# Moving the context's layer-1 top-k and the latents' filter into another stage, and pairing the latents' attention on the two halves of TensorE, in a two-layer backbone step

## The chip, the cores and the metric

The kernel runs on one NeuronCore of a Trainium2 chip. The metric is the device time of one execution in microseconds (us); lower is better. Below, DVE is VectorE, ACT is ScalarE, PE is TensorE's matmul side, POOL is GpSimd and SP is SyncE.

## The reference, cut to what matters

Two streams of tokens go through two layers with the same weights: the context (128 tokens, "C") and the latents (512 tokens, "L"). Layer 1 of a stream needs layer 0 of that stream and nothing of the other one.

```python
def layer(x, mod, P, rope, k_ext, v_ext):          # D=1024, 8 query heads, 2 kv heads, head_dim 64
    h = rmsnorm(x, norm_mix_g) * (1 + sc_m) + sh_m
    proj = h @ w_in
    attn = attention(q, k, v)                      # latents: 128 cached + 512 own keys; context: 128 keys
    hy   = hyena(proj[...], P)                     # long convolution; its filter depends on weights alone
    sg   = chunk_gmlp(proj[...])
    x = x + g_m * (concat([attn, hy, sg]) @ w_out)
    h = rmsnorm(x, norm_ffn_g) * (1 + sc_f) + sh_f
    return x + g_f * peer(h, ...)

def peer(h, wq, keys, u_tab, v_tab):               # 8 heads, 128 keys a half, top 16
    q = (h @ wq).reshape(T, 8, 2, 64)
    s = einsum('thpd,hpnd->thpn', q, keys)         # two rows of 128 scores per token and head
    s_top, i_top = top_k(s, 16)                    # of each half
    cand = s_top[..., 0, :, None] + s_top[..., 1, None, :]       # 16 x 16
    sc, pos = top_k(cand, 16)
    idx = i_top0[pos // 16] * 128 + i_top1[pos % 16]
    gate = softmax(sc)
    a = gelu(einsum('td,ted->te', x, u_tab[idx]))  # 128 rows of 4 KB per token from u_tab
    return einsum('te,ted->td', gate * a, v_tab[idx])            # and 128 from v_tab
```

The filter is `sin(fr2*(sin(fr1*(feats@fw1+fb1))@fw2+fb2))@fw3`, times an exponential, and its spectrum.

## The kernel before, in words

All engines follow one list, `ORDER`, that is worked out when the program is built; each engine does, in that order, what a job gives it, and waits on semaphores between. There are two kinds of jobs.

*Mixer jobs* are everything up to the scores: `rms`, `app` (norm and modulation), `f1`, `f2`, `f3`, `hf` (the filter: two sines, the taps, the spectrum), `qk`, `vt`, `hy`, `su` (projections), `rot`, `sp`, `df`, `cv`, the attention jobs `as` (scores), `at` (turning the probabilities with a diagonal matrix of 1/sum, line 823) and `av` (values, line 835), then `wo`, `wq`, and `ka`, `kb` (the two halves of the keys, line 865).

*Expert jobs* work in units. A unit is one head of one tile of 128 tokens, and in a unit each of the 128 partitions handles one token and its 16 experts. Step `u` of a group does for unit `u` 16 `dot` jobs (DVE, line 1415: a gathered row of u_tab times the token), for unit `u-1` 16 `add` jobs (the gathered row of v_tab times a weight), and for unit `u+1` the `pick` jobs, which are the top-k chain on DVE (lines 1358 to 1402, 27 instructions, each waiting for the one ahead). In the context's groups `add` is a DVE instruction (line 1429). In the latents' groups it is two matmuls with a diagonal matrix that ACT makes (lines 885 and 1113). Rows are gathered by POOL (line 610), one indirect DMA of 128 rows of 4 KB each, u and v in turn, into rings of four places each (`rows_ring`); a place is free when its `dot` or `add` is done.

The groups are context layer 0 (8 units), latents layer 0 (32), context layer 1 (8) and latents layer 1 (32). `weave` puts expert jobs between mixer jobs in proportion to a table `ROOM` of costs per mixer job. So the program has these stages:

1. context mixer of layer 0, alone;
2. latents mixer of layer 0, woven with the experts of context layer 0;
3. context mixer of layer 1, woven with steps 0 to 16 of latents layer 0;
4. steps 17 to 32 of latents layer 0, alone, and then `start_jobs(2)`: the picks of the first unit of context layer 1;
5. latents mixer of layer 1, woven with the experts of context layer 1. It begins `rms app f1 f2 f3 f3 f3 f3 hf hf hf hf qk ...`;
6. latents experts of layer 1, alone, and the outputs.

Weights come in blocks of 1 MB through a ring of four places that SP fills in the order in which they are used.

A softmax unit of the latents is one head of one tile of 128 queries: `n // (2 * NT)` is the pair of heads, and the half of the partitions (0 to 63 or 64 to 127) changes only every four units. Three units are in flight, each in two PSUM banks. `ROOM` gives 9 to each `as`, `at` and `av`, which is 864 for the 32 units; the whole list is 2964 in layer 0 and 3004 in layer 1.

## Time and profile before

| | |
|---|---|
| median of 3 runs | 4240.7 us (4236.87 to 4241.16) |
| the profiled execution, its own time | 4239.37 us |
| span of its instructions | 4237.5 us |
| mean granted TensorE clock (share of 2.4 GHz) | 0.934 |
| DVE busy in the span | 2951.7 us (70%) |
| PE busy | 3274.7 us (77%) |
| POOL busy | 2563.5 us (60%) |
| ACT busy | 1065.3 us (25%) |
| moved by DMA | 1485.64 MB, mean 351 GB/s |

The shares of busy time are means over six stages with different limits, so they say little by themselves. The windows of the profile, which give busy times and GB/s for stretches of the span, are what to read here.

### The profile page before, as it was taken

Reading aid. Unit: us, or ns where it says so; the run is one execution under the profiler, and the core shown is the slowest. Engines: PE = TensorE matmul, PEld = TensorE weight load, DVE = VectorE, ACT = ScalarE, POOL = GpSimd, SP = SyncE. Lnnn points to the kernel's source line nnn. Section 1 sums busy time; section 2 is a strip of 40 time slices with the busy share of each in tenths; the row PEclk is TensorE's granted clock in tenths of the full one; section 3 lists DMA queues with packets and bytes.
Section 4 is the critical chain, followed back from the end, with each engine's and each line's share of the span. In section 5 each row is a group of like instructions: output and inputs, shape, how many; then the busy total and the mean of one; then the engine's idle time right before and its main releaser. Section 6 shows DMA issues by size and latency. Waiting matters only on the chain.

```text
span 4237.5 us, 33926 instructions
## 1 busy us (share of the span) xinstructions
PE 3274.7 (77%) x9680; PEld 1513.7 (36%) x9680; DVE 2951.7 (70%) x6826; ACT 1065.3 (25%) x2256; POOL 2563.5 (60%) x2564
## 2 busy tenths in 40 slices
PE   6797896577778787777776978975777777777777
PEld 4653653233333333222222536542222222222223
DVE  2388998545667666677764889897676767677673
ACT  4322322122222222222223323221222222222222
POOL 0054666345656666777773545566777777777774
PEclk8898998689999999999998988987999999999999
DMA  7587788899989999999995877788999999999998
GB/s 281 215 314 276 262 297 287 330 378 369 381 332 384 379 407 386 408 409 401 409 407 191 318 277 244 275 303 336 409 407 395 407 409 400 409 406 401 401 409 313
DMA packets 394007, 1485.64 MB, mean 351 GB/s; under 512 B 44124, under 2 KB 46878, under 8 KB 377952
## 3 DMA queue, kind: packets, MB, share of 16 engines
q0 software_dynamic: 368640, 1342.34, 82.5%
q1 hardware_dynamic: 25184, 141.13, 8.6%
q8 instruction: 81, 1.33, 0.1%
q14 instruction: 102, 0.84, 0.1%
HBM read 1480.42 MB, written 2.88 MB: 350 GB/s over the span
## 4 chain that ended last, share of the span: by engine, by line
DMA 25%; DVE 21%; PE 19%; POOL 18%; issue 13%; ACT 4%; SPq 0%; DVEq 0%; ACTq 0%; POOLq 0%
POOL rows_ring L610 18%; DMA rows_ring<-in_peer_u,idx 13%; DMA rows_ring<-in_peer_v,idx 11%; PE psum L885 8%; DVE rows_ring L1415 7%; DVE mix L1429 4%; PE psum L700 4%; PE psum L687 1%; PE psum L823 1%; DVE small L1334 1%; PE psum L656 1%; DMA ring<-in_ada 1%; DVE pos L1362 1%; DVE pos L1359 1%; DVE cand L1360 1%
## 5 line engine op out<-in xcount | busy, mean ns | idle before, releaser
L885 PE MATMUL psum<-rows_ring,diag 128*128 128x512 f32 x4096 | 2042.7, 627 | 674.9 <-DMA rows_ring<-in_peer_v,idx 544.5
L610 POOL DMA_INDIRECT rows_ring<-in_peer_u,idx x1280 | 1298.0, 1014 | 1015.5 <-DVE rows_ring L1415 475.3
L1415 DVE SCALAR_TENSOR_TENSOR rows_ring<-rows_ring,psum 128x1024 f32<-128x1024 f32 x1024 | 1240.7, 1220 | 678.9 <-DMA rows_ring<-in_peer_u,idx 639.7
L610 POOL DMA_INDIRECT rows_ring<-in_peer_v,idx x1280 | 1265.2, 988 | 634.2 <-issue 306.6
L885 PEld LDWEIGHTS psum<-rows_ring,diag 128*128 128x128 f32 x4096 | 717.3, 193 | 1937.6 <-DMA rows_ring<-in_peer_v,idx 1231.7
L1113 ACT ACTIVATE diag<-ident,wts 128x128 f32<-128x128 f32 x1024 | 382.3, 397 | 1333.3 <-PE psum L885 1332.6
L700 PE MATMUL psum<-area,ring 128*128 128x128 f32 (+1 forms) x1344 | 386.7, 447 | 15.6 <-ACT area L975 14.9
L1429 DVE SCALAR_TENSOR_TENSOR mix<-rows_ring,wts,mix 128x1024 f32<-128x1024 f32 x254 | 326.4, 1285 | 15.5 <-DMA rows_ring<-in_peer_v,idx 13.9
L1415 DVE SCALAR_TENSOR_TENSOR rows_ring<-rows_ring,area 128x1024 f32<-128x1024 f32 x256 | 311.9, 1222 | 13.5 <-DMA rows_ring<-in_peer_u,idx 12.0
L700 PEld LDWEIGHTS psum<-area,ring 128*128 128x128 f32 x1344 | 216.3, 200 | 195.0 <-issue 191.7
L700 PE MATMUL psum<-mix,ring 128*128 128x128 f32 (+1 forms) x512 | 143.0, 441 | 2.9 <-DVE mix L1354 2.1
L1105 ACT ACTIVATE acts<-dots 128x16 f32<-128x16 f32 x80 | 17.3, 216 | 498.4 <-DVE rows_ring L1415 498.3
L823 PE MATMUL psum<-sg_junk,area 128*128 128x128 f32 x672 | 109.5, 314 | 37.0 <-DVE sg_junk L1343 37.0
L823 PEld LDWEIGHTS psum<-sg_junk,area 128*128 128x128 f32 x672 | 93.5, 214 | 53.8 <-DVE sg_junk L1343 43.5
L1101 ACT ACT_TABLE_LOAD x75 | 96.2, 1283 | 41.0 <-DVE wts L1440 41.0
L700 PEld LDWEIGHTS psum<-mix,ring 128*128 128x128 f32 x512 | 80.8, 198 | 67.3 <-issue 63.6
L835 PE MATMUL psum<-area,v_tok 128*64 128x128 f32 x672 | 102.4, 304 | 0.0
L1075 ACT ACTIVATE area<-psum,small 128x640 f32<-128x640 f32 (+1 forms) x80 | 56.9, 711 | 176.0 <-DVE small L1334 175.9
L1105 ACT ACT_TABLE_LOAD x78 | 100.1, 1283 | 1.4
L813 PE MATMUL psum<-area 64*128 64x512 f32 x128 | 81.6, 720 | 13.3 <-ACT area L1082 6.7
L1082 ACT COPY area<-psum 128x640 f32<-128x640 f32 (+1 forms) x80 | 48.5, 606 | 161.3 <-PE psum L823 161.3
L835 PEld LDWEIGHTS psum<-area,v_tok 128*64 128x64 f32 x672 | 81.4, 152 | 15.7 <-issue 9.3
(176 smaller groups left out, 2497.3 us busy)
## 6 DMA issues: line engine op xcount, KB each, us to landing
ring<-in_ada SPq DMA_DIRECT2D x48, 1024.0 KB, 8.2
ring<-in_win SPq DMA_DIRECT2D x32, 1024.0 KB, 8.1
rows_ring<-in_peer_u,idx POOLq DMA_INDIRECT x1280, 7.2
rows_ring<-in_peer_v,idx POOLq DMA_INDIRECT x1280, 7.1
ring<-in_wout SPq DMA_DIRECT2D x16, 1024.0 KB, 8.0
ring<-in_wq SPq DMA_DIRECT2D x16, 1024.0 KB, 7.8
ring<-in_dft SPq DMA_DIRECT2D x12, 1024.0 KB, 7.8
xT<-in_xT_in SPq DMA_DIRECT2D x1, 2048.0 KB, 13.1
```

What stands on the lines that cost most here:

```text
L610: pool.indirect_dma_start(row(table, k), None, (peer_u, peer_v)[table], bass.IndirectOffsetOnAxis(ap=idx[u % IDX_PLACES][:, k:k + 1], axis ...
L700: m = pe.matmul(g[:, 0:WIDTH[st]], w[:, k * P:(k + 1) * P], src(k), start=(k == 0), stop=(k == KC - 1))
L813: pe.matmul(g[:, 0:512], q, kT[st][rows, 0:512], start=True, stop=True)
L823: m = pe.matmul(att_bank(st, n)[:, b * P:(b + 1) * P], probs[st][:, n % 2, b * P:(b + 1) * P], softmax_diag[:, n % 2, :], start=True, stop ...
L835: m = pe.matmul(out_bank(st, c)[rows, t * P:(t + 1) * P], v_tok[:, b, rows], probsT[st][:, n % 2, i * P:(i + 1) * P], start=(i == 0), stop ...
L885: m = pe.matmul(acc[:, b, :], diag[:, k % 4, :], row(1, k)[:, b * 512:(b + 1) * 512], start=(u % PEER_HEADS == 0 and k == 0), stop=last)
L1075: act.activation(probs[st][:, n % 2, :], att_bank(st, n)[:, 0:KEYS[st]], ACT.Exp, bias=negmax[:, n % 2:n % 2 + 1], accum_out=rowsum[:, n % ...
L1101: act.activation(gate_e[:], best[:], ACT.Exp, bias=gate_s[:, 1:2], accum_out=gate_s[:, 0:1]).then_inc(s["gexp_ready"], 1)
L1105: act.activation(acts[:], dots[:], ACT.Gelu_apprx_tanh).then_inc(s["gelu_ready"], 1)
L1113: act.activation(diag[:, k % 4, :], ident[:], ACT.Copy, scale=wts[:, k:k + 1]).then_inc(s["diag_ready"], 1)
L1415: dve.scalar_tensor_tensor(out=row(0, k), in0=row(0, k), scalar=1.0, in1=h, op0=ALU.mult, op1=ALU.mult, accum_out=dots[:, k:k + 1]).then_i ...
L1429: m = dve.scalar_tensor_tensor(out=out_tok[C_], in0=x, scalar=wts[:, k:k + 1], in1=out_tok[C_], op0=ALU.mult, op1=ALU.add)
```

## The change

It has five parts.

- **Picks ahead.** In steps 18 to 25 of group 1 (latents layer 0) DVE also does the picks of the eight units of group 2 (context layer 1), one unit a step. Group 2 then has none of its own, and `start_jobs(2)` goes. Its indices and gates get places for all eight units.
- **Filter earlier.** `f1 f2 f3 hf` of the latents of layer 1 leave stage 5 and are woven into steps 25 to 32 of group 1, with buffers of their own.
- **Picks in eight parts.** A pick has 24 instructions instead of 27, in eight parts instead of six: the two one-hot halves are now one instruction of 512 elements each. It works on the scores themselves, and ACT's copy of them (`stage`) goes.
- **Attention by pairs.** The latents' softmax units go two at a time, one on each half of the partitions, so that neighbouring matmuls of the scores (64 rows) and of the values (64 columns) lie on different halves of the array. Two pairs are in flight instead of three units. The diagonal matrix of 1/sum moves from DVE to ACT. `ROOM` for it is now 10 + 20 + 10 per pair, 640 in all.
- **Keys by pairs.** `ka` and `kb` are one job on PE, the two halves in turn.

```diff
@@ attention_jobs
+    if st == L_:
+        n = ATT_UNITS[L_] // 2
+        jobs = [("fence", l, st, 0), ("pas", l, st, 0), ("pas", l, st, 1)]
+        for m in range(n):
+            jobs += [("pat", l, st, m)] + ([("pav", l, st, m - 1)] if m else [])
+            jobs += [("pas", l, st, m + 2)] if m + 2 < n else []
+        return jobs + [("pav", l, st, n - 1), ("fence", l, st, 1)]
@@ filter_jobs, mixer_jobs
+FILTER_FROM = 25
+def filter_jobs(l):
+    return [("f1", l, L_, 0), ("f2", l, L_, 0)] + [(k, l, L_, t) for k in ("f3", "hf") for t in range(LAT_TILES)]
-        jobs = js("rms:0 app:0 f1:0 f2:0") if l else []
-        jobs += js("f3:0 f3:1 f3:2 f3:3 hf:0 hf:1 hf:2 hf:3")
+        jobs = js("rms:0 app:0") if l else js("f3:0 f3:1 f3:2 f3:3 hf:0 hf:1 hf:2 hf:3")
@@ step_jobs, expert_jobs, ORDER
-PICK_LINKS = (0, 5, 10, 16, 20, 23, 27)
+PICK_LINKS = (0, 3, 5, 8, 10, 13, 16, 21, 24)
+PICK_AT = (0, 1, 3, 4, 6, 7, 9, 10)
+PICKED_AHEAD = (2,)
+AHEAD_FROM = 18
-        jobs += [("pick", grp, u + 1, p // 2)] if u + 1 < n and p % 2 and p // 2 < PICK_PARTS else []
+        if own and ahead and p < PICK_PARTS:
+            jobs += pick_jobs(grp, u + 1, [p])
+        elif own and not ahead and p in PICK_AT:
+            jobs += pick_jobs(grp, u + 1, [PICK_AT.index(p)])
+        if ahead and p >= PICK_PARTS:
+            jobs += pick_jobs(*ahead, [p - PICK_PARTS])
-    ORDER += expert_jobs(_g, range(_a, UNITS[_g] + 1))
-    if _l + 1 < DEPTH:
-        ORDER += start_jobs(_g + 1)
+        ORDER += expert_jobs(_g, range(_a, FILTER_FROM))
+        _a = FILTER_FROM
+        ORDER += weave(filter_jobs(_l + 1), expert_jobs(_g, range(_a, UNITS[_g] + 1)))
@@ TensorE
+            def pair_scores(l, st, m):
+                if m >= 2:
+                    pe.wait_ge(s["pair_copied"], 2 * done("pat", l, st, m - 2))
+                for n, a, b in ((2 * m, 512, 640), (2 * m + 1, 128, 640), (2 * m, 0, 512), (2 * m + 1, 0, 128)):
+                    c, rows, t = unit_of(st, n)
+                    if (a, b) == (0, 128):
+                        pe.wait_ge(s["pair_first"], done("pas", l, st, m))
+                    ins = pe.matmul(att_bank(st, n)[:, a:b], qT[st][rows, c, t * P:(t + 1) * P], kT[st][rows, a:b], start=True, stop=True)
@@ ScalarE, at "pat": exp of pair m+1, copy of pair m, diagonals of pair m+1
+                    act.activation(probs[st][m % 2][:, n % 2, :], att_bank(st, n), ACT.Exp, bias=negmax[:, n % 2:n % 2 + 1],
+                                   accum_out=rowsum[:, n % 2:n % 2 + 1]).then_inc(s["pair_exp"], 1)
+                    act.copy(probsT[st][:, n % 2, :], att_bank(st, n)).then_inc(s["pair_copied"], 1)
+                    act.activation(softmax_diag[:, n % 2, :], ident[:], ACT.Copy, scale=rinv[:, n % 2:n % 2 + 1]
+                                   ).then_inc(s["pair_diag"], 1)
@@ VectorE, pick
-                if part < 2:
-                    top16(topv[:, part, :], topi[:, part, :], unit_s[:, part, :], step)
+                if part < 4:
+                    half = part // 2
+                    src = scores[st][:, (2 * u + half) * N_KEYS:(2 * u + half + 1) * N_KEYS]
+                    if part % 2 == 0:
+                        top8(vals, idxs, src, step)
+                        step(dve.match_replace(src, vals[:, 0:8], src, -3.0e38))
+                    else:
+                        next8(vals, idxs, src, step)
```

On DVE, the end of stage 4 and the start of stage 5 read so before (`xT` is the last write of the latents' experts, `unit_s` the first unit of group 2, line 1402 its indices, line 1169 the norm, lines 1198 to 1203 the first sine's argument):

```order
L1451 SCALAR_TENSOR_TENSOR xT<-psum,modT,xT 128x128 x8
L1358 MAX topv<-unit_s 128x8
L1359 MAX_INDEX topi<-topv,unit_s 128x8
...
L1400 SCALAR_TENSOR_TENSOR idxf<-picked 128x16
L1402 TENSOR_SCALAR idx<-idxf 128x16
L1169 TENSOR_TENSOR area<-xT,rstd 128x512 x8
L1415 SCALAR_TENSOR_TENSOR rows_ring,dots<-rows_ring,area 128x1024
L1198 TENSOR_SCALAR area<-psum,par 64x512
```

The changed kernel has there (line 1560 is the `dot`, line 1343 the first key's gain):

```order
L1597 SCALAR_TENSOR_TENSOR xT<-psum,modT,xT 128x128 x8
L1289 TENSOR_TENSOR area<-xT,rstd 128x512 x8
L1560 SCALAR_TENSOR_TENSOR rows_ring,dots<-rows_ring,area 128x1024 x2
L1343 TENSOR_SCALAR area<-psum,par 128x512
L1560 SCALAR_TENSOR_TENSOR rows_ring,dots<-rows_ring,area 128x1024 x9
```

The pick of 27 instructions and the filter's instructions are gone from this place, and the norm follows the last write of `xT`.

In step 25 of group 1 the changed kernel's DVE has both additions; `xT` is the last tile's write back, `sq` the second sine's argument, `gate_l` belongs to the latents' own pick:

```order
L1597 SCALAR_TENSOR_TENSOR xT<-psum,modT,xT 128x128 x8
L1490 MAX topv<-area 128x8
...
L1491 MAX_INDEX pos<-best,onehot 128x8
L1318 TENSOR_SCALAR sq<-psum,par 64x512
L1319 TENSOR_SCALAR sq<-sq 64x512
L1320 TENSOR_SCALAR sq<-sq 64x512
L1322 SCALAR_TENSOR_TENSOR sq<-sq 64x512 x3
L1323 TENSOR_SCALAR sq<-sq 64x512
L1560 SCALAR_TENSOR_TENSOR rows_ring,dots<-rows_ring,psum 128x1024
L1531 MATCH_REPLACE onehot<-best,onehot 128x256
```

Before, a step held 16 dots, one pick and `weigh`; steps 18 to 25 now hold 16 dots and two picks, and step 25 also the write back, both sines' arguments and the first of four `f3`.

On PE the latents' attention read before (813 and 814 scores, 823 the turn, 835 the values), one unit after another:

```order
L813 MATMUL psum<-area 128x512
L814 MATMUL psum<-area 128x128
L823 MATMUL psum<-sg_junk,area 128x128 x5
L835 MATMUL psum<-area,v_tok 64x128 x5
L813 MATMUL psum<-area 128x512
```

and now (891 scores, 900 the turn, 913 the values), one pair after another:

```order
L891 MATMUL psum<-area 128x128
L891 MATMUL psum<-area 128x512 x2
L891 MATMUL psum<-area 128x128
L900 MATMUL psum<-sg_junk,area 128x128 x10
L913 MATMUL psum<-area,v_tok 64x128 x10
```

The number of matmuls per unit is the same; what moved is which half of the array neighbours use, and that two units wait and are waited for together.

## Rows read from the trace of the kernel before

**Rows 1.** The page: GB/s that DMA moved, in 40 equal slices.

```profile
GB/s 281 215 314 276 262 297 287 330 378 369 381 332 384 379 407 386 408 409 401 409 407 191 318 277 244 275 303 336 409 407 395 407 409 400 409 406 401 401 409 313
```

**Rows 2.** Windows by stage: stretch, length, each engine's busy us and instructions, clock, DMA.

```profile
core 0: us, PE busy (x) PEld busy (x) DVE busy (x) ACT busy (x) POOL busy (x), PEclk, DMA share, GB/s
207.00:760.00 553.00, 455.49 (x1733) 275.61 (x1733) 487.22 (x924) 146.93 (x250) 322.23 (x260) 0.88 0.79 282
1510.00:2276.00 766.00, 599.72 (x1333) 221.23 (x1331) 505.50 (x1232) 173.38 (x406) 541.17 (x571) 0.99 1.01 398
2276.00:2868.00 592.00, 482.40 (x1778) 287.25 (x1779) 512.46 (x989) 168.84 (x281) 309.25 (x260) 0.87 0.74 264
```

**Rows 3.** Windows of pieces of stage 5, and of stage 2's attention (last).

```profile
2276.00:2351.00 75.00, 40.40 (x108) 22.45 (x109) 53.17 (x140) 26.10 (x37) 17.93 (x16) 0.70 0.31 99
2351.00:2530.00 179.00, 157.74 (x494) 85.71 (x493) 155.82 (x293) 52.70 (x82) 93.52 (x81) 0.94 0.83 305
2530.00:2700.00 170.00, 144.80 (x772) 109.24 (x773) 154.63 (x315) 57.44 (x109) 93.73 (x78) 0.85 0.73 251
2700.00:2824.00 124.00, 116.32 (x265) 50.26 (x264) 113.26 (x178) 25.45 (x39) 81.49 (x72) 0.97 0.90 342
2824.00:2868.00 44.00, 23.14 (x143) 19.58 (x142) 35.58 (x66) 7.15 (x14) 22.58 (x17) 0.62 0.64 210
419.00:577.00 158.00, 136.83 (x768) 103.61 (x768) 153.65 (x318) 57.60 (x109) 97.99 (x77) 0.89 0.77 265
```

**Rows 4.** Timeline of DVE around the end of stage 4: start us, us, engine, line.

```profile
2284.16 0.28 DVE L1358 MAX8 topv<-unit_s 128x8 f32<-128x128 f32 x1
...
2294.67 0.17 DVE L1402 TENSOR_SCALAR idx<-idxf 128x16 uint32<-128x16 f32 x1
...
2303.99 0.69 DVE L1169 TENSOR_TENSOR area<-xT,rstd 128x512 f32<-128x512 f32 x1 [9.14 <-ACT rstd L967]
```

**Rows 5.** Timeline of DVE in stage 5: a dot, the first sine's argument, and what follows.

```profile
2308.82 1.22 DVE L1415 SCALAR_TENSOR_TENSOR rows_ring<-rows_ring,area 128x1024 f32<-128x1024 f32 x1
...
2309.96 0.80 DVE L1198 TENSOR_SCALAR area<-psum,par 64x512 f32<-64x512 f32 x1
...
2314.20 1.21 DVE L1415 SCALAR_TENSOR_TENSOR rows_ring<-rows_ring,area 128x1024 f32<-128x1024 f32 x1
```

**Rows 6.** Groups of DVE instructions in 2276 to 2868: xcount | busy, mean ns.

```profile
L1429 DVE SCALAR_TENSOR_TENSOR mix<-rows_ring,wts,mix 128x1024 f32<-128x1024 f32 x127 | 163.1, 1284 | 6.4 <-DMA rows_ring<-in_peer_v,idx 5.3
L1334 DVE TENSOR_REDUCE small<-psum 128x1 f32<-128x640 f32 x32 | 26.3, 821 | 9.6 <-PE psum L814 9.5
L1343 DVE TENSOR_SCALAR sg_junk<-ident,small 128x128 f32<-128x128 f32 x32 | 9.9, 311 | 1.1
L1215 DVE TENSOR_TENSOR x<-psum,tmp 128x512 f32<-128x512 f32 x4 | 2.8, 689 | 0.1
```

**Rows 7.** Groups of ACT instructions in 2276 to 2868.

```profile
L1075 ACT ACTIVATE area<-psum,small 128x640 f32<-128x640 f32 x32 | 25.5, 796 | 82.1 <-DVE small L1334 82.0
L1082 ACT COPY area<-psum 128x640 f32<-128x640 f32 x32 | 22.1, 691 | 62.5 <-PE psum L823 62.5
```

**Rows 8.** Groups of matmuls in 2276 to 2868: busy (overlaps counted once), mean ns.

```profile
L823 PE MATMUL psum<-sg_junk,area 128*128 128x128 f32 x320 | 51.3, 315 | 17.5 <-DVE sg_junk L1343 17.5
L835 PE MATMUL psum<-area,v_tok 128*64 128x128 f32 x320 | 47.7, 304 | 0.0
L813 PE MATMUL psum<-area 64*128 64x512 f32 x64 | 41.7, 735 | 8.2 <-ACT area L1082 5.4 <-DVE mix L1311 2.9
L687 PE MATMUL psum<-area,ring 128*128 128x256 f32 x128 | 32.7, 421 | 5.3 <-issue 5.3
L767 PE MATMUL psum<-sgwT,sg_v 128*64 128x128 f32 x32 | 2.2, 279 | 0.0
```

**Rows 9.** Window of one step of latents layer 0, alone (stage 4).

```profile
1752.20:1793.10 40.90, 31.71 (x65) 10.84 (x64) 29.12 (x73) 9.47 (x22) 30.66 (x33) 1.00 1.03 409
```

**Rows 10.** Waits in 1668.9 to 2000.5: who waited for what, us, times, longest.

```profile
POOL rows_ring L610 <- issue: 70.5, 222, 1.9
```

More of the change, by code:

```diff
@@ L168, with pick_jobs, step_jobs @@
 PIECES = TOPK // PER_PIECE
-PICK_LINKS = (0, 5, 10, 16, 20, 23, 27)
+PICK_LINKS = (0, 3, 5, 8, 10, 13, 16, 21, 24)
 PICK_PARTS = len(PICK_LINKS) - 1
-def step_jobs(grp, u):
+PICK_AT = (0, 1, 3, 4, 6, 7, 9, 10)
+PICKED_AHEAD = (2,)
+AHEAD_FROM = 18
+def pick_jobs(grp, u, parts=range(PICK_PARTS)):
+    return [("pick", grp, u, p) for p in parts]
+def step_jobs(grp, u, ahead=None):
     n, jobs = UNITS[grp], []
+    own = u + 1 < n and grp not in PICKED_AHEAD
     latent = GROUPS[grp][1] == L_
@@ L197, in expert_jobs @@
 def expert_jobs(grp, steps):
-    return [job for u in steps for job in step_jobs(grp, u)]
+    out = []
+    for u in steps:
+        v = u - AHEAD_FROM
+        early = grp + 1 in PICKED_AHEAD and 0 <= v < UNITS[grp + 1]
+        out += step_jobs(grp, u, (grp + 1, v) if early else None)
+    return out
 def start_jobs(grp):
-    return [("stage", grp, 0, 0)] + [("pick", grp, 0, p) for p in range(PICK_PARTS)] + [("gexp", grp, 0, 0)]
+    return pick_jobs(grp, 0) + [("gexp", grp, 0, 0)]
 def weave(mixer, experts):
@@ L241 @@
     _count[_job[0]] = NUMBER[_job] + 1
+    if _job[0] == "pick":
+        PICK.setdefault(_job[1:3], len(PICK))
+LAST_GEXP, _last = {}, {}
+for _job in ORDER:
+    if _job[0] == "pick" and _job[3] == 4:
+        LAST_GEXP[_job[1:3]] = _last.get(GROUPS[_job[1]][1])
+    elif _job[0] == "gexp":
+        _last[GROUPS[_job[1]][1]] = _job
 def done(*job):
@@ L264, in bank_choice @@
         return range(4, 8) if GROUPS[a][1] == L_ else range(2, 8)
-    return range(4, 8) if b == C_ else range(2, 8)
+    return range(4, 8) if b == C_ or (kind in ("f1", "f2", "f3", "hf") and a) else range(2, 8)
 BANK, BANK_BEFORE, FENCE_BEFORE, _turn, _last = {}, {}, {}, 0, {}
@@ L447, in mixer_peer_kernel @@
         topf = grid(sb("topf", 2 * TOPK)[:, :], 2)
-        best = sb("best", TOPK)
+        best = [sb(f"best{st}", TOPK) for st in (L_, C_)]
         pos = sb("pos", TOPK, U32)
@@ new lines, in pair_turn, with pair_values @@
+            def pair_turn(l, st, m):
+                pe.wait_ge(s["pair_diag"], 2 * done("pat", l, st, m))
+                for n in (2 * m, 2 * m + 1):
+                    for b in range(KEYS[st] // P):
+                        ins = pe.matmul(att_bank(st, n)[:, b * P:(b + 1) * P], probs[st][m % 2][:, n % 2, b * P:(b + 1) * P],
+                                        softmax_diag[:, n % 2, :], start=True, stop=True)
+                ins.then_inc(s["pair_turned"], 1)
+            def pair_values(l, st, m):
+                pe.wait_ge(s["pair_copied"], 2 * done("pat", l, st, m))
+                c, _, t = unit_of(st, 2 * m)
+                if t == 0 and c >= 2:
+                    pe.wait_ge(s["attn_ready"], attended(l, st, c - 2))
+                blocks = [TILES, 0, 1, 2, 3]
+                for i, b in enumerate(blocks):
+                    for n in (2 * m, 2 * m + 1):
+                        _, rows, _ = unit_of(st, n)
+                        ins = pe.matmul(out_bank(st, c)[rows, t * P:(t + 1) * P], v_tok[:, b, rows], probsT[st][:, n % 2, i * P:(i + 1) * P],
+                                        start=(i == 0), stop=(i == len(blocks) - 1))
+                ins.then_inc(s["pair_out"], 1)
@@ L851, in tok, with keys_of @@
                 m.then_inc(s["tok_mm"], 1)
-            def key(l, st, i, g, half):
+            def keys_of(l, st, i, g):
                 t, h0 = i // 2, 4 * (i % 2)
-                if i == 0 and half == 0:
+                other = BANK_BEFORE["kb", l, st, i]
+                pe.wait_ge(s[READ[other[0]]], read_value(other))
+                out = (g, psum[:, BANK["kb", l, st, i], :])
+                if i == 0:
                     if st == C_:
@@ L862, in key @@
                 a = COLS[st].start + t * P
-                rows = slice(64 * half, 64 * half + 64)
                 for h in range(4):
-                    m = pe.matmul(g[:, h * P:(h + 1) * P], mix[rows, h0 + h, a:a + P], keys[rows, h0 + h, :],
-                                  start=True, stop=True)
-                m.then_inc(s[("ka_mm", "kb_mm")[half]], 1)
+                    for half, rows in ((0, slice(0, 64)), (1, slice(64, P))):
+                        m = pe.matmul(out[half][:, h * P:(h + 1) * P], mix[rows, h0 + h, a:a + P], keys[rows, h0 + h, :],
+                                      start=True, stop=True)
+                        if h == 3:
+                            m.then_inc(s[("ka_mm", "kb_mm")[half]], 1)
             def ht(grp, l, t, half, g):
@@ L1103, in weigh @@
+                act.activation(gate_e, best[GROUPS[grp][1]][:], ACT.Exp, bias=gate_s[:, 1:2], accum_out=gate_s[:, 0:1]
+                               ).then_inc(s["gexp_ready"], 1)
             def weigh(g):
```

224 lines of the change are left out of this document (140 added, 84 removed).

## Prediction

> **What bounds the kernel now.** I read the page's slices first. DMA moves 386 to 409 GB/s from the 15th slice to the 21st and 395 to 409 from the 29th to the last but one, and 191 to 336 in the seven between [rows 1]. So there are stretches in which DMA is full, and stretches in which something else paces. The windows by stage say which is which. Stage 4 (1510 to 2276) moves 398 GB/s at a DMA share of 1.01, and one of its steps takes 40.9 us with DVE busy for 29.1 [rows 2, 9]: gathers pace it, DVE has about 11 us free a step. Stage 5 (2276 to 2868) takes 592 us at 264 GB/s with DVE busy for 512 (87%) and PE for 482 (81%); stage 2 is like it, 553 us and DVE 487 [rows 2]. These two are paced by DVE, with PE close behind. The reader is to see in rows 2 that the same top-k instruction is almost free in stage 4 and costs its full length in stages 2 and 5.
>
> Then I cut stage 5 into pieces [rows 3]. In the first 75 us DMA moves 99 GB/s and PE is busy for 40: latency, not load. In the projections (179 us) PE is busy 158 and DVE 156. In the attention (170 us) DVE is busy 155 and PE 145. In wo and wq (124 us) PE is busy 116, DVE 113, and DMA's share is 0.90. Last come the keys, 44 us.
>
> **How expert work is spread.** `weave` deals it out by ROOM, so I need DVE time per unit of ROOM in stage 5. A dot holds DVE for 1.14 us (2308.82 to 2309.96) [rows 5], an add for 1.28 [rows 6]: 128 of each is 310 us, and `weigh` makes it about 319. A pick takes from 2284.16 to 2294.84, 10.7 us [rows 4]; seven of them are 75. Before: 394/3004 = 0.131 us per unit of ROOM. After: the picks are gone and ROOM is 3004 - 180 (filter) - 224 (attention) = 2600, so 319/2600 = 0.123. As a test, attention before should hold 864 x 0.131 = 113 us of experts, and 26.3 + 9.9 us of maxima and diagonals [rows 6], and about 8 of reciprocals and copies: 157, where the window shows 154.6 [rows 3].
>
> **Stage 5, start: 50 us off.** The last write back ends at 2284.16, where the pick of unit 0 begins; ACT's exp for its gate stands ahead of the norm's squares and waits for the pick's best scores, which come about two thirds into it; the norm's first product is at 2303.99 [rows 4]. Without the pick I take it 7 us earlier, at 2297. `app` streams behind it, so `qk:0` can run from about 2301. Before, PE came to it only at 2351, after the sines, `f3` and `hf` [rows 3]. 50 us.
>
> **Projections: 5 us off.** PE's load is unchanged (158 us). DVE's falls from 156 by 960 x 0.008 = 8. Two engines at nearly the same load gave 179 us; I take 174.
>
> **Attention: 45 us off.** ROOM 640 x 0.123 = 79 us of experts, 4.9 us for each of 16 pairs. DVE also does two maxima (1.64) and two reciprocals (0.3) a pair. ACT has two exps (1.6, about 2.0 with their sums), two copies (1.4) [rows 7] and now two diagonals (0.8, my estimate from DVE's 0.31 each in [rows 6]). In order, DVE does the maxima of pair m+1, then a quarter of the experts (1.2 us), and then must wait for that pair's exps (2.1) before the reciprocals, so a pair costs DVE 1.64 + 2.1 + 0.3 + 3.65 = 7.7 us; 16 are 123. ACT's 4.2 and PE's turn fit under it. On PE the scores' 512 columns take 42 us, their last 128 some 12 by the share of columns, the values 48 [rows 8], of 145. If neighbouring halves run together these halve, and PE has some 95. How sure is that? The spatial products of L767 have the values' shape and do alternate halves: 32 take 2.2 us, 69 ns each; the values, which stay on one half, take 47.7/320 = 149 ns [rows 8]. So I take 125 us instead of 170.
>
> **wo and wq: 4 us worse.** Here POOL comes in. A gather holds it for 81.49/72 = 1.13 us in this stretch, 1.20 in the attention, against 541/571 = 0.95 in stage 4 [rows 2, 3], and 0.32 us passes before the next [rows 10]. ROOM 884 x 0.123 is 109 us of rows work, 44.7 pairs of rows, 89 gathers x 1.45 = 129 us, more than PE's 116. I take 128 for 124.
>
> The Trainium skill (SBUF — State Buffer, Who interferes with whom) says that a DVE instruction with two SBUF inputs contends with a GpSimd instruction that reads SBUF. The longer gathers above agree with it: in stage 5 the dot reads its token from SBUF, in stage 4 from PSUM. That rule speaks against this change, because one-hot products and the candidates' sum have two SBUF inputs and go into the stage that gathers pace; with two picks a step it would add at most their length, some 2 x 1.8 us, to a step of 40.9, which is 8 x 3.6 = 29 us, where the row of one step with one such pick (0.95 us a gather) makes it under 3.
>
> **Keys: 4 us off** (40 for 44): half the matmul time of the small products, while the two copies and the pick of group 3 stay.
>
> Stage 5: 25 + 174 + 125 + 128 + 40 = 492 against 592, **100 us off**. As a floor, DVE alone needs 512 - 82 (eight picks) - 15 (the filter) - 10 (diagonals) = 405.
>
> **Stage 2: 15 us off.** Seven picks of about 10 us remain and ROOM falls from 2964 to 2740: (319 + 70)/2740 = 0.142 for 0.133. Attention: 91 us of experts, 5.7 a pair, 8.3 us a pair by the same count, 133 for 158 [rows 3]: 25 off. The other 2100 of ROOM get 0.009 each, 19 us of DVE, of which I let about 14 show (wo, wq 8, projections 4, rest 2), and 4 come back in the keys.
>
> **Stage 4: 15 us worse.** A pick of 24 linked instructions is about 10 us (10.7, less 0.55 for the one-hots and three links). A step with two: 16 x 1.14 + 20 + 0.8 = 39 of 40.9 us. That fits, without room: 3 us for the seven ordinary ones. Step 25 is different. It adds the write back (2.2 us and a wait) and two sines' arguments, each 2309.96 to 2314.20 = 4.2 us [rows 5] with a wait for PE and ACT between, and an `f3` of 1.4 (0.69 of it in [rows 6]): about 54 us. Four places in each ring hide perhaps 4 of the 13 over, so 9 to 10 are lost. An `hf` is 16 of the 128 instructions that take 32.7 us [rows 8], so 4.1 us of PE at a time, against its 9 us of idle in a step [rows 9]; the rings hide it. The two weight blocks that follow `hf` now load here, 2 to 3 us. Bounds: 3 (all hidden) and 50 (two picks a step as slow as 3 us over each, and 25 us at the filter).
>
> Stage 1, 3 and 6 keep their work. **Sum:** 4239.4 - 100 - 15 + 15 = 4139 in the profiled execution's own time, which is 1.3 us under the median: **4140 us**.
>
> **Rivals.**
> - *The halves don't run together* (0.13). Then the scores and values keep their 104 us, PE keeps 145 in the attention, and it paces: 150 us a layer for 125 and 133. 25 + 17 worse: 4182. For it: scores of two halves also share a bank for 128 columns and wait on a semaphore. Against it: L767.
> - *The pair chain paces* (0.12). Two pairs in flight hold as many units as before, but ACT's exp, copy and diagonals, PE's turn and the next scores follow each other with DVE's experts in between. At 9.5 us a pair, 152 a layer, it costs 27 + 19: 4186.
> - *Steps 18 to 25 lose more* (0.12): DVE at 95% with 40 short waits a step, gathers stretched. 7 x 3 us and 20 more at the filter: 4181.
> - *No difference* (0.03): stage 5 gets its time from gathers after all. 256 x 1.45 = 371 us is the floor of POOL, so this needs everything else to go wrong too: 4240.
> - *Slower* (0.05): the attention of both layers waits on DVE's queue. Each job there stands in one line with dots whose rows must land, and a pair that misses its turn stalls PE and ACT together. It decides from the point where 32 pairs lose what the rest gains: the rest is 100 + 15 - 15 - 70 = 30 us, about 1 us each. Two units take 10.6 us today in layer 1 (170/16) and 9.9 in layer 0, so a pair would have to take over 11.2 on average. 4250.
> - My forecast 0.55.
>
> **How the numbers follow.** The forecast is the likeliest case. Its own range is 4110 to 4165: stage 4 between 3 and 40 worse, the pieces of stage 5 each within 10 us. The range for 8 in 10 reaches up over the three cases at 4181 to 4186 and down to 4105: 4105 to 4195. Faster by over 0.2% (8 us, about what a measurement can tell from no change) 0.92, within 0.2% 0.03, slower 0.05.
>
> **What would show it.** Per step: in the windows, stage 5 from the last write of `xT` to the first step of group 3 in about 492 us with over 300 GB/s; PE on `qk:0` some 17 us after that write. Attention of layer 1 in about 125 us, with the scores and values under 60 us of PE busy. Steps 18 to 24 at 41 to 42 us each, step 25 at about 50. Wrong would be steps of 44 and more with waits of POOL on dots, an attention over 150 us with DVE waiting for PE or ACT, or a wait of PE in stage 5 for something that I hold to be ready (the filter, weights). A lower granted clock in the attention than 0.85 would mean that less work on PE made each matmul longer.

## The result and the profile after

The changed kernel takes 4171.64 us (median of 4 runs, 4163.25 to 4175.58) where the kernel before takes 4238.78 (4 runs on the same chips). The ratio is 0.9842, 95% interval 0.9821 to 0.9863: 67 us faster, where 100 were forecast and 45 to 135 allowed. Below, times are compared in the profiled executions, 4237.5 us of span before and 4161.4 after; 76 us lie between these two, since the profiled execution of the changed kernel was the fastest of its four.

The page's slices of the changed kernel, GB/s, to be held against [rows 1]:

```profile
GB/s 283 225 315 287 249 298 308 355 381 363 387 351 389 369 403 399 401 381 354 363 392 370 264 321 309 340 274 379 408 406 399 409 406 399 409 408 397 410 408 309
```

The dip in the middle has lost its deepest slice (191, now 264), and the plateau ahead of it, 401 to 409 before, now has 381, 354, 363 and 392: something was gained behind the 22nd slice, and something was lost ahead of it.

Windows of the changed kernel, cut where pieces begin and end: steps 17 to 31 of group 1; its tail to the last write of `xT`; then stage 5's start (norm), projections, attention, wo and wq, keys.

```profile
core 0: us, PE busy (x) PEld busy (x) DVE busy (x) ACT busy (x) POOL busy (x), PEclk, DMA share, GB/s
1600.90:2261.40 660.50, 504.00 (x1059) 189.78 (x1058) 508.20 (x1324) 148.53 (x345) 451.94 (x476) 0.96 0.99 384
2261.40:2298.00 36.60, 32.05 (x76) 12.82 (x75) 2.39 (x9) 7.21 (x17) 16.34 (x18) 1.00 0.79 264
2298.00:2312.40 14.40, 9.09 (x17) 3.22 (x17) 1.77 (x3) 9.79 (x14) 0.00 (x0) 0.88 0.01 1
2312.40:2500.80 188.40, 159.03 (x493) 85.81 (x494) 156.74 (x235) 49.77 (x75) 114.89 (x96) 0.93 0.84 315
2500.80:2621.30 120.50, 85.35 (x768) 72.77 (x768) 108.17 (x172) 62.39 (x135) 77.36 (x66) 0.94 0.87 304
2621.30:2755.30 134.00, 121.73 (x274) 52.22 (x272) 112.93 (x146) 21.08 (x32) 94.91 (x80) 0.95 0.93 351
2755.30:2796.30 41.00, 16.12 (x144) 14.19 (x144) 33.63 (x66) 7.34 (x12) 19.21 (x16) 0.64 0.63 214
```

The same pieces in the kernel before, cut at the same events (the first `weigh` of a step, the first and last matmul of a piece, the last piece at the first dot of stage 6), are steps 17 to 31 in 622.1 us, tail 36.6, start 66.8, projections 180.5, attention 166.1, wo and wq 129.4, keys 43.5. So:

| piece | before | after | difference | forecast |
|---|---|---|---|---|
| up to step 16 (stages 1 to 3) | 1625.5 | 1600.9 | -24.6 | -15 |
| steps 17 to 31 | 622.1 | 660.5 | +38.4 | +15 |
| tail of stage 4 | 36.6 | 36.6 | 0 | 0 |
| start of stage 5 | 66.8 | 14.4 | -52.4 | -50 |
| projections | 180.5 | 188.4 | +7.9 | -5 |
| attention, layer 1 | 166.1 | 120.5 | -45.6 | -45 |
| wo, wq | 129.4 | 134.0 | +4.6 | +4 |
| keys | 43.5 | 41.0 | -2.5 | -4 |
| stage 6 | 1367.0 | 1365.1 | -1.9 | 0 |

The attention's matmuls in the changed kernel (2500 to 2625), to be held against [rows 8]:

```profile
L900 PE MATMUL psum<-sg_junk,area 128*128 128x128 f32 x320 | 42.8, 292 | 7.9 <-ACT sg_junk L1202 7.9
L891 PE MATMUL psum<-area 64*128 64x512 f32 x64 | 23.5, 678 | 0.0
L913 PE MATMUL psum<-area,v_tok 128*64 128x128 f32 x320 | 21.0, 278 | 1.4 <-ACT area L1197 1.4
```

The mean of one changed little (735 and 678 ns, 304 and 278), but the busy time, which counts overlaps once, fell from 41.7 to 23.5 us and from 47.7 to 21.0. Where the mean stays and the busy time falls, matmuls ran at the same time. A part of the fall is the clock, whose mean over the attention was 0.85 before and is 0.94 now: with single units at 0.95 (below) the same two groups are busy for 37.0 and 42.7 us.

Where stage 4 lost its time can be read in three windows of the changed kernel: one ordinary double step, step 25, and a step with one `hf`.

```profile
1684.70:1727.60 42.90, 32.34 (x64) 11.76 (x64) 37.38 (x105) 9.46 (x23) 30.13 (x33) 0.96 1.01 391
1941.90:2001.30 59.40, 38.13 (x80) 14.75 (x78) 49.28 (x131) 14.35 (x29) 31.70 (x34) 0.86 0.84 295
2044.20:2087.10 42.90, 33.69 (x81) 13.98 (x80) 28.61 (x69) 9.32 (x22) 30.92 (x33) 1.00 0.99 385
```

The step with `hf` has DVE busy for 28.6 of 42.9 us and is still 2 us over its 40.9. And the waits of the changed kernel in the seven double steps ahead of step 25 (1641.8 to 1941.9: who waited for what, us, times, longest):

```profile
POOL rows_ring L680 <- PE psum L984: 19.0, 15, 3.7
PE psum L984 <- ACT diag L1225: 18.1, 7, 3.2
ACT L1212 <- DVE wts L1586: 11.9, 7, 1.9
```

Seven waits of about 2.6 us, one per step: PE stands without a diagonal where the weights of a new unit come in. The granted clock has a share in what this costs. Its mean over steps 18 to 24 is 0.96, where it was 1.00 before: after PE's wait of 3.02 us that ends at 1687.46, for one, the granted clock from 1688.2 to 1691.7 is 0.51, its lower level (1.2 GHz).

### The profile page after: what moved, and what is told of

Its sections match the earlier page's. It is cut to its first block, busy times and chain, and to the rows that moved or that the text cites. A ratio compares the mean times of both kernels' runs of the same rounds, so it can differ in the third digit from the quotient of the medians.

```text
span 4161.4 us, 33677 instructions
## 1 busy us (share of the span) xinstructions
PE 3145.0 (76%) x9680; PEld 1439.0 (35%) x9680; DVE 2890.9 (69%) x6522; ACT 1039.7 (25%) x2232; POOL 2554.8 (61%) x2564
## 4 chain that ended last, share of the span: by engine, by line
DMA 30%; PE 19%; POOL 17%; DVE 16%; issue 12%; ACT 4%; SPq 0%; DVEq 0%; ACTq 0%; POOLq 0%
DMA rows_ring<-in_peer_v,idx 19%; POOL rows_ring L680 17%; PE psum L984 10%; DMA rows_ring<-in_peer_u,idx 8%; DVE rows_ring L1560 5%; DVE mix L1574 3%; PE psum L770 3%; DMA rows_ring<-in_peer_v,idx_c 1%; PE psum L757 1%; DMA rows_ring<-in_peer_u,idx_c 1%; DVE small L1475 1%; ACT area L1189 1%; DMA ring<-in_ada 1%; PE psum L726 1%; PE psum L719 1%
## 5 line engine op out<-in xcount | busy, mean ns | idle before, releaser
L984 PEld LDWEIGHTS psum<-rows_ring,diag 128*128 128x128 f32 x4096 | 726.9, 194 | 1944.9 <-DMA rows_ring<-in_peer_v,idx 1159.3
L680 POOL DMA_INDIRECT rows_ring<-in_peer_u,idx x1024 | 976.9, 954 | 478.4 <-issue 271.5
L680 POOL DMA_INDIRECT rows_ring<-in_peer_v,idx x1024 | 968.9, 946 | 485.8 <-PE psum L984 277.6
L680 POOL DMA_INDIRECT rows_ring<-in_peer_u,idx_c x256 | 322.3, 1259 | 433.7 <-DVE idx_c L1547 202.6
L680 POOL DMA_INDIRECT rows_ring<-in_peer_v,idx_c x256 | 286.6, 1119 | 185.1 <-DVE mix L1574 128.8
L900 PE MATMUL psum<-sg_junk,area 128*128 128x128 f32 x640 | 91.5, 305 | 19.0 <-ACT sg_junk L1202 19.0
L1189 ACT ACTIVATE area<-psum,small 128x640 f32<-128x640 f32 x64 | 50.3, 790 | 197.7 <-DVE small L1475 197.7
L891 PE MATMUL psum<-area 64*128 64x128 f32 (+1 forms) x256 | 47.5, 497 | 62.4 <-ACT area L1197 57.4
L900 PEld LDWEIGHTS psum<-sg_junk,area 128*128 128x128 f32 x640 | 85.3, 216 | 23.7 <-ACT sg_junk L1202 19.8
L1560 DVE DVE_READ_ACCUMULATOR rows_ring<-rows_ring,psum 128x1 f32 x1024 | 84.6, 83 | 0.0
```

What stands on the lines that cost most here:

```text
L680: pool.indirect_dma_start(row(table, k), None, (peer_u, peer_v)[table], bass.IndirectOffsetOnAxis(ap=idx_of(grp, u)[:, k:k + 1], axis=0)). ...
L891: ins = pe.matmul(att_bank(st, n)[:, a:b], qT[st][rows, c, t * P:(t + 1) * P], kT[st][rows, a:b], start=True, stop=True)
L900: ins = pe.matmul(att_bank(st, n)[:, b * P:(b + 1) * P], probs[st][m % 2][:, n % 2, b * P:(b + 1) * P], softmax_diag[:, n % 2, :], start=T ...
L984: m = pe.matmul(acc[:, b, :], diag[:, k % 4, :], row(1, k)[:, b * 512:(b + 1) * 512], start=(u % PEER_HEADS == 0 and k == 0), stop=last)
L1189: act.activation(probs[st][m % 2][:, n % 2, :], att_bank(st, n), ACT.Exp, bias=negmax[:, n % 2:n % 2 + 1], accum_out=rowsum[:, n % 2:n % 2 ...
L1560: dve.scalar_tensor_tensor(out=row(0, k), in0=row(0, k), scalar=1.0, in1=h, op0=ALU.mult, op1=ALU.mult, accum_out=dots[:, k:k + 1]).then_i ...
```

## The experiments

Each was timed against the kernel before in its own chip's runs, so it is the ratio that compares; for the changed kernel it is 0.9842 (0.9821 to 0.9863). 0.001 is 4.2 us.

### One part undone at a time

**Picks back in stage 5.**

```diff
-PICKED_AHEAD = (2,)
+PICKED_AHEAD = ()
+        ORDER += start_jobs(_g + 1)
```

The added line stands behind the last step of group 1.

> The changed kernel, with the eight context picks of layer 1 back in their own experts (the first one alone at the end of stage 4). Theory (the picks' DVE time is what stages 2 and 5 are paced by): stage 5 gets some 8 x 10 us of DVE back, less what gathers already hold, so 55 to 80 us longer there, and steps 18 to 24 go from 42.9 us back to 41.3, so 11 us less; the filter's step 25 falls from 59 us to about 50. Net 40 to 60 us slower than the changed kernel, 4210 to 4230 us. Rival (gathers pace stage 5 already, the picks there were free): 10 to 20 us faster than the changed kernel.

4220.71 us, ratio 0.9970 (0.9953 to 0.9987): 54 us slower than the changed kernel. From `weigh` of step 31 to the end of the keys it takes 597.8 us (2246.9 to 2844.7) where the changed kernel takes 534.9, and steps 17 to 31 take 13 us less. The picks ahead are most of the gain: 63 us in, 13 us out. The rival, that gathers pace stage 5 anyway, falls. Step 25 takes 55.0 us without a second pick (50 were expected), so of the 17 us that it lost, 12 are the filter's and 4 the second pick's.

**Filter back in the mixer.**

```diff
-        jobs = js("rms:0 app:0") if l else js("f3:0 f3:1 f3:2 f3:3 hf:0 hf:1 hf:2 hf:3")
+        jobs = js("rms:0 app:0 f1:0 f2:0") if l else []
+        jobs += js("f3:0 f3:1 f3:2 f3:3 hf:0 hf:1 hf:2 hf:3")
-        ORDER += expert_jobs(_g, range(_a, FILTER_FROM))
-        _a = FILTER_FROM
-        ORDER += weave(filter_jobs(_l + 1), expert_jobs(_g, range(_a, UNITS[_g] + 1)))
+        ORDER += expert_jobs(_g, range(_a, UNITS[_g] + 1))
...
```

The lines left out give the filter its old buffers back.

> The changed kernel, with f1, f2, f3 and hf of the latents of layer 1 back in stage 5. Theory: the start of stage 5 is longer by the chain of sines and spectrum, about 42 us, and steps 25 to 31 lose what they gained in length, 17 + 13 us, so it is only 5 to 20 us slower than the changed kernel: 4175 to 4192 us. Rival (the chain at the start is worth its full 42 us because the filter's cost in stage 4 comes from the picks ahead of it): 35 us or more slower, over 4205 us.

4170.13 us, ratio 0.9859 (0.9833 to 0.9884), not to be told from the changed kernel. Steps 17 to 31 take 633.8 us in place of 660.5, and the rest of the stretch to the end of the keys 564.5 in place of 534.9. By these windows the filter's move costs 27 us where it goes and saves 30 where it was.

**Single units in the attention** (scores, turn, values, diagonals, ROOM and keys as before the change).

```diff
-            c, t, half = n // 2 // NT[st], n // 2 % NT[st], n % 2
+            c, half, t = n // (2 * NT[st]), n // NT[st] % 2, n % NT[st]
-    if st == L_:
-        n = ATT_UNITS[L_] // 2
-        jobs = [("fence", l, st, 0), ("pas", l, st, 0), ("pas", l, st, 1)]
...
-        return jobs + [("pav", l, st, n - 1), ("fence", l, st, 1)]
```

> The changed kernel, with the latents' attention and the keys as in the kernel before (single units, three in flight, DVE's diagonals, ROOM 864). Theory: the attention goes from 120 and 136 us back to about 150 and 157, and what ROOM then takes from the other pieces gives 10 to 15 us back: 30 to 45 us slower than the changed kernel in all, 4200 to 4217 us. Rival (the attention only got shorter because ROOM moved its experts elsewhere): the sum of the stages is the same, within 10 us.

4187.47 us, ratio 0.9886 (0.9863 to 0.9910): 19 us slower by the ratios, less than expected. The attention of layer 1 takes 141.2 us (2511.5 to 2652.7), not 150, since its share of the experts no longer holds picks; of the 21 us more in it the other pieces of stage 5 give most back, and 9 us of the difference arise in stage 2 and 6 in stage 3. That the missing picks make it shorter is argued; DVE is busy for 135 us in it, where it was for 151 before.

**Pairs, but one half's matmuls ahead of the other's.**

```diff
-                for n, a, b in ((2 * m, 512, 640), (2 * m + 1, 128, 640), (2 * m, 0, 512), (2 * m + 1, 0, 128)):
+                for n, a, b in ((2 * m, 0, 512), (2 * m, 512, 640), (2 * m + 1, 128, 640), (2 * m + 1, 0, 128)):
-                for i, b in enumerate(blocks):
-                    for n in (2 * m, 2 * m + 1):
+                for n in (2 * m, 2 * m + 1):
+                    for i, b in enumerate(blocks):
```

(and likewise in the keys.)

> The changed kernel with the same pairs, but all matmuls of one half ahead of those of the other, in scores, values and keys, so that neighbours share a half. Theory A (the halves' running together is worth time): scores and values take about 100 us of PE busy in the attention of layer 1 again instead of 59, PE nears 130 of it, and the attention goes from 120 to 135 us or more; 20 to 35 us slower in all. Theory B (DVE and the pair chain pace it, PE had room): PE is busy for as long, but the attention stays within 6 us and the total within 12 us of the changed kernel.

4206.19 us, ratio 0.9937 (0.9914 to 0.9960): 40 us slower than the changed kernel, and slower than single units too. The window of its attention of layer 1, its values and its scores there (both widths together), and its waits:

```profile
2519.60:2662.40 142.80, 114.81 (x768) 95.49 (x768) 109.05 (x172) 63.42 (x135) 79.33 (x68) 0.87 0.77 264
```

```profile
L913 PE MATMUL psum<-area,v_tok 128*64 128x128 f32 x320 | 32.3, 278 | 1.4 <-ACT area L1197 1.4
L891 PE MATMUL psum<-area 64*128 64x512 f32 (+1 forms) x128 | 31.4, 509 | 23.1 <-ACT area L1197 20.0 <-DVE mix L1431 2.2
```

```profile
ACT area L1197 <- PE psum L913: 30.7, 15, 4.6
DVE small L1475 <- PE psum L891: 13.7, 10, 2.4
```

The time is on the side of theory A (40 us for 20 to 35), its numbers aren't. Values and scores are busy for 32.3 + 31.4 = 63.7 us, not for 100, and PE for 115 of 143 us, not for 130. So PE isn't full, and the halves still run together in part when they are in turn (with single units the two take 42.7 + 44.0 = 86.7 us). Against the changed kernel's 21.0 + 23.7 = 44.7 us they take 19 us more, 1.2 a pair. The turn's matmuls, whose order is the same, take 53.1 us for 42.8; the mean granted clock is 0.87 here and 0.94 there. DVE's work is what it was (109.1 and 108.2 us); it now waits for PE's scores (13.7 us; 0.8 in the changed kernel). Mixing the halves takes PE's time off the chain from one pair's copy to the next scores' maxima, 19 us of the attention's 22.3, if all of it shows there; how much of the difference is the lower clock, and why it is lower, was not taken apart. In layer 0 the attention takes 145.0 us for 135.6, so some 8 of the 40 us lie in other pieces.

### Where stage 4 loses

**Filter one step later.**

```diff
-FILTER_FROM = 25
+FILTER_FROM = 26
```

> The changed kernel with the filter woven into steps 26 to 32 instead of 25 to 32. Theory (step 25 is long because two picks, a write back and two sines meet on DVE, and ACT waits in line for the sine's argument): step 25 falls from 59 to 44 us, step 26 rises from 43 to about 47, the rest is as it was: 8 to 12 us faster than the changed kernel. Rival (the time goes to the filter's own waits wherever it stands): step 26 takes 55 us or more and the total is within 5 us.

4172.43 us, ratio 0.9854 (0.9829 to 0.9879): not to be told from the changed kernel. Steps 25 and 26 take 46.6 and 51.3 us for 59.4 and 42.9, steps 25 to 31 together 319.9 for 319.5. The rival holds in the sum, though step 26 stays under its 55 us: the filter costs the same at either place.

**Pick parts early in a double step.**

```diff
-        if own and ahead and p < PICK_PARTS:
-            jobs += pick_jobs(grp, u + 1, [p])
...
-        if ahead and p >= PICK_PARTS:
-            jobs += pick_jobs(*ahead, [p - PICK_PARTS])
+LAST_PICK = 13
...
+        if own and ahead:
+            for i in range(2 * PICK_PARTS):
+                if i * LAST_PICK // (2 * PICK_PARTS) == p:
+                    jobs += pick_jobs(grp, u + 1, [i]) if i < PICK_PARTS else pick_jobs(*ahead, [i - PICK_PARTS])
```

> The changed kernel with the 16 pick parts of a double step dealt over its first 13 rows instead of 16, the same instructions. Theory A (a double step is longer because DVE is late at its last dot, so the weights, and with them ACT's diagonals and PE's adds, come late): with three rows free of picks at the end DVE catches up, steps 18 to 24 go from 42.9 to 41.5 us or less, 8 to 12 us faster in all. Theory B (DVE's load of 37 to 39 us against 40.9, or gathers made longer by DVE's port use, is the cause): the steps stay at 42.5 or more, no difference within 5 us.

4160.68 us, ratio 0.9823 (0.9799 to 0.9847). Steps 18 to 24 take 41.1 to 42.0 us, 291.6 together for 300.1. Theory A: the same steps, and PE's wait for a diagonal in them.

```profile
1649.80:1941.40 291.60, 222.83 (x457) 76.82 (x457) 260.70 (x728) 65.92 (x159) 212.08 (x224) 1.00 1.02 403
```

```profile
PE psum L985 <- ACT diag L1226: 6.3, 7, 1.1
```

DVE's work is the same to half a microsecond. Only its last dot of the step came in time, so the waits for the first diagonal fell from 18.1 to 6.3 us. With them the mean clock went from 0.96 back to 1.00 and PE's busy time from 230.3 to 222.8 us, so how much of the 8.5 us is the wait and how much the slower adds behind it stays open. The total is 8 us less with intervals that overlap; what makes the effect clear is that it repeats: steps 18 to 24 take 291.4 to 292.2 us in the six kernels with early parts, and 296.8 to 301.7 in the six with late ones.

**ACT's part of the filter later in its line** (and the filter from step 26).

```diff
...
+        if job[0] in ("f1", "f2", "hf") and job[1:3] == (1, L_):
+            held.append((LATE if job[0] == "hf" else 2, (job[0] + "_late", *job[1:])))
...
```

`LATE` is 4: ACT lets so many adds pass before it takes up an `hf`, and two before an `f1` or `f2`.

> As the filter from step 26, and in addition ACT's part of each filter job stands later in its line: the sines two adds, the copies of the spectrum four adds behind PE's matmuls. Theory (ACT stands in line before PE's spectrum, up to 13 us, makes no diagonals meanwhile, and so each spectrum costs 3 us): steps 27 to 31 go from 43.4 to about 41.3 us, 8 to 12 us faster than the filter from step 26 alone, 16 to 24 faster than the changed kernel. Rival (PE's 4.1 us per spectrum itself costs the time, by places of the ring that come free late): no more than 4 us against the filter from step 26.

4158.43 us, ratio 0.9826 (0.9801 to 0.9851). Steps 25 to 31 take 309.3 us, 10.6 less than with the filter from 26 alone; 5.1 us of it lie in step 26, where the sines stand, and 5.7 in steps 27 to 31 (10 were expected there). The greater waits are those at the sines. On PE, line 738 is `f1` and 742 `f2`; with the filter from 26 alone, the adds behind them read

```profile
2000.92 11.32 PE L984 MATMUL psum<-rows_ring,diag 128*128 128x512 f32 x20 [5.77 <-ACT diag L1225]
2019.02 3.75 PE L984 MATMUL psum<-rows_ring,diag 128*128 128x512 f32 x4 [5.79 <-ACT diag L1225]
```

and with ACT's part late

```profile
1994.96 3.67 PE L1002 MATMUL psum<-rows_ring,diag 128*128 128x512 f32 x8 [1.63 <-ACT diag L1243]
2014.48 3.94 PE L1002 MATMUL psum<-rows_ring,diag 128*128 128x512 f32 x8 [1.11 <-ACT diag L1243]
```

An `hf` costs less. One of the four in the changed kernel, on ACT:

```profile
2110.21 0.59 ACT L1100 COPY area<-psum 128x512 f32<-128x512 f32 x1 [13.25 <-PE psum L757]
```

ACT came to the copy of the spectrum 13.25 us ahead of PE, because it works up to four adds ahead, and stood there; so PE, when it had the spectrum, found no diagonal for its next add. It waited 1.07 us for one behind three of the four spectra and 2.77 behind the last, where ACT had a gate's exp to do as well, and not 3 us at each as expected. With ACT's part late these waits are gone.

**Both** (below, the early-and-late kernel).

```diff
-FILTER_FROM = 25
+FILTER_FROM = 26
+LAST_PICK = 13
+LATE = 4
```

With these, the two edits above, unchanged.

> All three together: filter from step 26, ACT's part later, picks in the first 13 rows. If the effects are separate they add: 22 to 34 us faster than the changed kernel, some 4132 to 4145 us where before is 4233. If DVE's lateness only moves from one step to the next, it equals the late-ACT kernel within 5 us.

4153.16 us, ratio 0.9811 (0.9787 to 0.9835). Steps 17 to 31 take 645.4 us for 660.5, 15.1 us less, where the early picks alone took off 8.4 and the late ACT 12.4: the two effects add for the greater part in this stretch. In the total it is 13 us by the ratios, less than the 22 to 34 expected, and not to be told from either of the two alone.

### The spread of the experts, and the last versions

**ROOM of a pair 52 and 28 instead of 40**, on top of the early-and-late kernel.

```diff
-        "pas": 10, "pat": 20, "pav": 10,
+        "pas": 13, "pat": 26, "pav": 13,
```

That is 52; for 28 they are 7, 14 and 7.

> The early-and-late kernel with ROOM 13, 26, 13 for a pair's jobs instead of 10, 20, 10 (832 in all for 640), so that more expert work lies in the latents' attention and less in projections, wo and wq. Theory (the attention is paced by DVE, wo and wq by gathers and DMA, the projections by both and PE): each us of DVE moved costs one in the attention and gives back about one elsewhere, 1.1 where gathers pace: attention of layer 1 some 17 us longer, total within 6 us. Rival (the projections' 188 us come from experts that are too dense there): 8 us or more faster.

> The same with ROOM 7, 14, 7 (448 in all). The pair chain then shows: with 3.6 us of experts a pair in place of 4.9, exps, copies, diagonals, turn and scores (some 6.5 us a pair) pace the attention, which gets shorter by less than what is moved out, while wo and wq, already paced by gathers, take more: 8 to 20 us slower. Rival (experts anywhere cost the same): within 5 us.

With 52: 4162.89 us, ratio 0.9844 (0.9818 to 0.9871), 14 us slower by the ratios where 6 at most were expected. The attention of layer 1 takes 132.2 us for 123.6, the projections 183.3 for 188.5, so moving the experts neither helps nor does it hurt beyond the interval. With 28: 4189.79 us, ratio 0.9900 (0.9880 to 0.9921), much slower than expected. Its attention takes 123.6 us in layer 1 and 123.3 in layer 0. In layer 1 that is no shorter than in the kernel that it was made from, though DVE is busy for 92.0 us in it and not for 108.5; so there 123.6/16 = 7.7 us is about what a pair's chain takes by itself (the changed kernel has 7.5, at a mean clock of 0.94 for 0.92). In layer 0 it is 11 us shorter (134.3), and the rest of stage 2 gets longer by more.

**The filter in the mixer, picks early:** the edits of the filter back in the mixer and of the early pick parts, together.

> The kernel with the filter back in stage 5, with the picks in the first 13 rows of a double step. Theory: the early picks give their 7 us here too, and the filter in stage 4 with ACT's part late is worth about 10 us over this: 4160 to 4166 us where before is 4233. Rival (the filter's move is worth nothing in either form): equal to the early-and-late kernel within 3 us.

4164.78 us (4156.97 to 4175.08), ratio 0.9851 (0.9827 to 0.9876). By the windows it saves 19.7 us in steps 17 to 31 against the early-and-late kernel (625.7 for 645.4) and loses 20.1 from there to the end of the keys. Its ratio is 0.0040 higher, with intervals that overlap, so by the windows the filter's move is worth nothing in its late form, by the ratios some 17 us, and the 10 us expected are neither shown nor excluded.

**One step earlier**, against the early-and-late kernel.

```diff
-AHEAD_FROM = 18
-FILTER_FROM = 26
+AHEAD_FROM = 17
+FILTER_FROM = 25
```

> The early-and-late kernel with the double steps at 17 to 24 and the filter from step 25. Theory (what the filter costs in stage 4 is its own length where DVE and PE are short of room, and two blocks of weights): step 25 has one pick and the write back, the filter has eight steps for seven, so 2 to 6 us less in steps 25 to 31, total 0.979 to 0.982 of before. Rival (the early double step meets the keys of the context and loses what the rest gains): the same as early-and-late within 2 us.

4141.76 us (4137.74 to 4151.65), ratio 0.9784 (0.9764 to 0.9804). This is the fastest kernel of the study, 94 us under the one before and about 25 under the changed one. Steps 17 to 31 take 641.7 us, 3.7 less than with early-and-late: steps 25 to 31 take 303.8 for 312.9, and step 17, now double, 46.1 for 41.1. So theory and rival both hold in part. The other 8 us of the ratio are not in that stretch and lie within what two runs differ by; the intervals of the two kernels overlap.

The shorter pick (24 instructions for 27, no copy by ACT) was not undone by itself, nor were the keys by pairs.

## Why the prediction was right, and where it was off

**The sum.** The profiled executions differ by 76 us for 100, the medians by 67. The forecast's own range, 4110 to 4165, was missed by 7 us; 4171.64 lies in the range for 8 in 10 because that range reaches up over the rivals. Two terms were off against the change, stage 4 by 23 us and the projections by 13, and stages 1 to 3 gave 10 more than was forecast, of which some can be luck (below).

**Stage 5's start, the attention, wo and wq, the keys.** These hold to within 3 us each, and stage 5 from the last write of `xT` takes 498 us for 492. `qk:0` starts 14.4 us after the last write of `xT`, where it started 66.8 after it. The attention takes 120.5 us for a predicted 125, and the count of a pair (7.7 us: maxima, the wait for the exps, reciprocals, three quarters of the experts) is met by the 7.5 us of a pair, but not for the reason that the forecast gave: in the kernel with ROOM 28 the pair chain, which the forecast put at ACT's 4.2 us with PE's turn under it, takes 7.7 us with DVE idle for a quarter of the time. So the step "ACT's 4.2 and PE's turn fit under it" was wrong, and that the number came out right was luck: DVE's count and the chain happen to be of one length. That the changed kernel stands just where the two meet is argued from these lengths.

**The rivals on the attention.** That the halves don't run together falls: the values take 21.0 us of PE for 47.7 before and 42.7 with single units at about the same clock. The forecast priced that case at 42 us, by a full PE. The kernel with the halves in turn measured 40 us, but it isn't that case: its halves run together in part, and its PE is idle for a fifth of the attention. That the pair chain paces is half true: it is the floor of the attention of layer 1, not at 9.5 us a pair but at 7.7. The granted clock, which the forecast feared to see under 0.85, rose to 0.94.

**Stage 4 is the term that was mis-sized:** 38 us for 15. The split by steps: 18 to 24 lost 11 us (3 forecast; they take 41.9 to 44.0 us each, where 41 to 42 were to be seen), step 25 17 us (9 to 10 forecast), 26 to 31 13 us (2 to 3 forecast), and step 17 gained 2.5. The forecast counted DVE's load (39 of 40.9 us) and PE's (4.1 of 9 us) and let the rings hide the rest. Both loads are about right (37.4 us of DVE in a double step, 3.62 of PE for an `hf`). What it left out are two hand-overs in line: DVE's last dot of a step, behind which stand weights, diagonals and adds, and ACT's place in line ahead of PE's `hf` and DVE's sine arguments. The first is shown by the early picks (same work, 8.5 us less in seven steps), the second by ACT's late part (10.6 us less), half of it at the sines. The forecast had the sines as work and waits of DVE, not as waits of PE. The rival that had steps 18 to 25 lose more (4181) gets 23 of its 41 us, and its reason is right only in part: DVE is late at the end of a step, but gathers weren't stretched, and the early parts gave the time back with DVE's load as it was. In step 31, which takes 5.7 us longer than before (46.6 for 40.9; 45.9 to 47.5 in all kernels with the filter in stage 4, and 40.9 in the two without), most of that is the weights: SP issues two 1 MB blocks at 2220.04, and the step moves 46.6 x 409 = 19.1 MB where it moved 40.9 x 406 = 16.6, at a full DMA share in both. At 409 GB/s two blocks take 5.1 us; the forecast had 2 to 3. The rest of what the filter costs was not taken apart.

**Gathers.** In the double steps a gather holds POOL for 0.95 us on average (215.70/227), as before. The Trainium skill (SBUF — State Buffer, Who interferes with whom) says that a DVE instruction with two SBUF inputs contends with a GpSimd instruction that reads SBUF. Nothing of that shows in these gathers, though the picks' instructions with two such inputs doubled, and the 29 us that the forecast worked out for it didn't come: with early parts the seven double steps take 291.6 us, 2.7 more than single ones did. In wo and wq it is 94.91/80 = 1.19 us, and the piece got 4.6 us longer, as forecast.

**Projections:** the sign was wrong, +7.9 for -5. The forecast took 8 us off DVE's load; it is 156.7 us for 157.3, since 92 dots and adds lie in the piece where 76 did, and they fill what the picks left. In the changed kernel all three of DMA (0.84 of its share over the piece, 1.01 from 2352 to 2432), PE (159 us) and DVE (157 us) are close together there. Thinner experts (ROOM 52) brought it back by 5 us and the attention took it again; denser ones (ROOM 28, 99 dots and adds) made it 11 us longer. Which of the three ends the waits isn't settled.

**Up to step 16** 24.6 us were gained for 15 forecast: 16 in stage 2, which is the forecast, and 4 each in stages 1 and 3, where nothing of weight changed; kernels that are alike in those stages differ by more (step 16 ends between 1597 and 1608 us in the nine that are), so against this run of the kernel before the gain there is anything from 18 to 28 us.

## What to carry to other kernels

Work moved into a stage that is paced by transfers is free only while it keeps the hand-overs of that stage: count the engine's load, but also ask what stands behind the last instruction of each round, and put the moved work early in the round. When an engine runs ahead of another in a common order, let it take up the other's result later in its own line by as much as it runs ahead. And before giving a long chain another place, price the place: by the windows 27 us there bought 30 here, and the two kernels' times can't be told apart.
